# Down-projection weights loaded with two neighbouring rows per partition, and the transposes of the hidden rows read every second column

## The reference

```python
xe = jax.vmap(lambda hb, ib: hb[ib])(h, idx)              # the rows that the expert chose
a = jnp.einsum('becd,edf->becf', xe, w_gate)              # w_gate (16, 1024, 1024)
u = jnp.einsum('becd,edf->becf', xe, w_up)                # w_up   (16, 1024, 1024)
ye = jnp.einsum('becf,efd->becd', jax.nn.silu(a) * u, w_down) * gate[..., None]
```

## Time and profile before

| | before |
|---|---|
| median of three executions | 2377.05 us |
| profiled execution, first to last instruction | 2376.4 us |
| TensorE busy | 2258.4 us (95%) |
| VectorE busy | 1758.0 us (74%) |
| ScalarE busy | 1272.3 us (54%) |
| DMA, whole kernel | 529.15 MB in 167652 packets |
| mixtures (without their edges) | about 745 to 1350 us and 1755 to 2350 us |

### The profile page before, as it was taken

One profiled execution on the slowest core, in us unless ns is written; L12 is line 12 of the kernel. 1 busy time (PEld: TensorE's weight loads), 2 busy tenths in 40 slices (PEclk: granted clock), 3 DMA queues, 4 the chain that ended last, 5 costly groups with the idle time before them and its releaser, 6 DMA issues.

```text
span 2376.4 us, 27238 instructions
## 1 busy us (share of the span) xinstructions
PE 2258.4 (95%) x10012; PEld 1547.3 (65%) x10012; DVE 1758.0 (74%) x1949; ACT 1272.3 (54%) x1348; POOL 194.6 (8%) x226
## 2 busy tenths in 40 slices
PE   7999999999988999999999798999979999999995
PEld 2867868768654666666666455777646666666663
DVE  4684765757767898999999534545378989999996
ACT  4212212213135777787777434444457778877773
POOL 1000000000022010111000110000120101110001
PEclk9999999999998999999999899999999999999997
DMA  7533434525345999999999310001269999999991
GB/s 271 159 117 115 142 107 158 159 92 166 107 177 205 341 354 348 364 360 342 350 339 360 117 39 1 36 1 37 98 235 346 352 345 359 362 354 343 338 353 59
DMA packets 167652, 529.15 MB, mean 223 GB/s; under 512 B 13525, under 2 KB 22282, under 8 KB 167306
## 3 DMA queue, kind: packets, MB, share of 16 engines
q1 hardware_dynamic: 162954, 515.35, 60.4%
q0 software_dynamic: 2304, 8.39, 1.0%
q10 hardware_dynamic: 2304, 4.20, 0.5%
HBM read 516.72 MB, written 11.17 MB: 222 GB/s over the span
## 4 chain that ended last, share of the span: by engine, by line
PE 90%; DVE 4%; ACT 3%; issue 1%; POOL 1%; DMA 0%; SPq 0%; POOLq 0%; ACTq 0%; DVEq 0%
PE ps L1751 86%; PE ps L1754 4%; ACT W_HI L338 0%; DVE IDX L1446 0%; DVE B L1273 0%; DVE X L1274 0%; ACT W L338 0%; DMA REGION<-in_ada_b_dram 0%; DVE MIXREG L1445 0%; ACT B L766 0%; POOL SMALL L608 0%; DVE ROUTE L1448 0%; ACT QN_HI L338 0%; POOL SMALL L607 0%; ACT GATE L940 0%
## 5 line engine op out<-in xcount | busy, mean ns | idle before, releaser
L1483 DVE TENSOR_TENSOR W_LO<-RAW_W,W_HI 128x2048 fp32r<-128x2048 f32 x384 | 867.4, 2287 | 76.3 <-ACT W_HI L338 72.5
L338 ACT ACTIVATE W_HI<-RAW_W 128x2048 fp32r<-128x2048 f32 x384 | 726.4, 1916 | 193.2 <-PE ps L1751 192.2
L1751 PE MATMUL ps<-W_HI,XET_HI 128*80 128x512 f32 x1024 | 322.3, 396 | 7.4 <-DVE B L1517 5.8
L1751 PE MATMUL ps<-W_HI,XET_LO 128*80 128x512 f32 x1024 | 319.7, 394 | 0.0
L1751 PE MATMUL ps<-W_LO,XET_HI 128*80 128x512 f32 x1024 | 319.5, 393 | 0.0
L1751 PEld LDWEIGHTS ps<-W_HI,XET_HI 128*80 128x80 f32 x1024 | 150.9, 148 | 89.1 <-DVE B L1517 6.7
L1751 PEld LDWEIGHTS ps<-W_LO,XET_HI 128*80 128x80 f32 x1024 | 152.0, 148 | 85.8 <-issue 1.0
L1751 PEld LDWEIGHTS ps<-W_HI,XET_LO 128*80 128x80 f32 x1024 | 151.9, 148 | 84.6 <-issue 0.9
L1230 DVE SCALAR_TENSOR_TENSOR ADA_SUM<-ADA_RAW,NCOL,ADA_SUM 128x512 f32<-128x512 f32 x280 | 191.2, 745 | 0.2 <-DMA ADA_RAW<-in_ada_w_dram 0.2
L1751 PE MATMUL ps<-W_HI,HTE_HI 128*80 128x512 f32 x512 | 167.0, 407 | 8.6 <-issue 8.6
L1751 PE MATMUL ps<-W_LO,HTE_HI 128*80 128x512 f32 x512 | 161.2, 396 | 0.0
(11 more groups left out here) (270 smaller groups left out, 3480.7 us busy)
## 6 DMA issues: line engine op xcount, KB each, us to landing
RAW_W<-in_moe_w_gate_dram SPq DMA_DIRECT2D x128, 1024.0 KB, 5.6
RAW_W<-in_moe_w_up_dram SPq DMA_DIRECT2D x128, 1024.0 KB, 6.0
RAW_W<-in_moe_w_down_dram SPq DMA_DIRECT2D x128, 1024.0 KB, 5.2
ADA_RAW<-in_ada_w_dram SPq DMA_DIRECT2D x80, 512.0 KB, 3.6
RING_RAW<-in_ret_w_in_dram SPq DMA_DIRECT2D x48, 512.0 KB, 4.7
W<-in_ada_w_dram SPq DMA_DIRECT2D x4, 2048.0 KB, 14.2
RING_RAW<-in_ret_w_out_dram SPq DMA_DIRECT2D x16, 512.0 KB, 4.7
xn_rows<-B SPq DMA_DIRECT2D x8, 512.0 KB, 12.7
```

The lines of the kernel that those rows point to most:

```text
L338: return nc.scalar.activation(out, in_, ACT.Copy, scale=scale)
L1483: V_.tensor_tensor(W_LO[:, slot], RAW_W[:, slot], W_HI[:, (place + i) % HSLOTS].bitcast(F32), ALU.subtract).then_inc(MS_["lo"], 1)
L1751: return T.matmul(out, lhsT, rhs, start=first, stop=last)
```

## The change

The load of a down unit takes its rows in another order: row 256q + 2p + k goes to partition p, block k. Two neighbouring rows of the matrix, 8192 bytes in a row in HBM, now go to one partition. Gate and up units are loaded as before. To match it, transpose c of `hidden_tr` reads the columns of `HID` that belong to the rows of its half unit: 256(c // 2) + 2p + c % 2 for p from 0 to 127, every second column of a block of 256. What is summed is the same, in another order.

```diff
@@ mix_load
-                src = a[("moe_w_gate", "moe_w_up", "moe_w_down")[w]][layer].rearrange("e (q k p) n -> e q p k n", p=P, k=2)
+                rows = "e (q p k) n -> e q p k n" if w == 2 else "e (q k p) n -> e q p k n"
+                src = a[("moe_w_gate", "moe_w_up", "moe_w_down")[w]][layer].rearrange(rows, p=P, k=2)
@@ hidden_tr
                     pe.wait_ge(MS_["h"], b["h"] + e + 1)
+                    pairs = HID[0:ROWS, :].rearrange("r (q p k) -> r q k p", p=P, k=2)
                     for c in range(KD):
-                        last = tr(ps[:, 6 + c // 4, (c % 4) * ROWS:(c % 4 + 1) * ROWS], HID[0:ROWS, c * P:(c + 1) * P], ROWS)
+                        last = tr(ps[:, 6 + c // 4, (c % 4) * ROWS:(c % 4 + 1) * ROWS], pairs[:, c // 2, c % 2, :], ROWS)
```

## The result

| | before | changed |
|---|---|---|
| median of the executions | 2377.78 us (4) | 2389.19 us (4) |
| lowest to highest | 2372.39 to 2378.69 us | 2388.51 to 2390.41 us |
| profiled execution, span | 2376.4 us | 2388.6 us |

A forecast was written before the change was run, and what follows sets the result against it. TensorE was taken to bound the kernel: 2376.4 us profiled, + 0 for transposes, - 0 to 1 for loads, gives 2376, and with 0.65 us from span to median 2377 us. The range was 2369 to 2389 us.

The forecast's parts named there:

- What bounds the kernel: Mixture windows: TensorE, busy all 400 us, sets the pace; SP's load queue waited 320.7 us for it, nothing on transfers.
- The loads: 128 down loads in 8192-byte pieces: 16384 packets fewer, landing hidden with 4.6 us spare, 0 to 1 us gained.
- the 6.2 forecast: Sign in the changed profile: down loads landing after 6.2 us or less, beside other loads at 6.0.
- the 0.2 us less for each down load: Landing of each 1024 KB down load in 8192-byte pieces: 0.2 us sooner, worth nothing on the path.
- the 0.4 us: Two 2048 KB loads outside the mixtures: 7.5 us in 8192-byte pieces against 7.9 in 4096, basis for the down loads.
- The transposes: Eight per `hidden_tr`, 32 groups: strided weight load taken as zero cost under the 0.070 us pass, 0.009 us spare.
- The upper end: Stride of two halves the weight load's rate: 0.122 us, 0.052 us more for seven transposes per group, 11.6 us.
- The first rival: Strided weight load in `hidden_tr` outlasts the pass covering it; at half rate 2389 us; chance 0.13.
- The other rivals: Products relieved of load writes, 2354 or 2369 us, faster side 0.05; slower load stream becoming the bound, 2396 us, 0.02.

The follow-up runs named there:

- e4_split_on_act_and_dve: Changed kernel's paired loads, but ACT and DVE read PSUM at every second column so transposes read neighbours; 2376.39 us, ratio 0.9993 against the kernel before.

## Why the prediction was wrong

**What bounds the kernel.** Right. TensorE was busy for 400 of 400 us and SP waited for it, before and after the earlier trace rows, which is why 0.35 us added to a group of transposes came through as 0.35 us of time.

**The loads.** Right on the path: packets as forecast, no wait for them, and alone 1.0007 with an interval that holds 1. That a down load landed after 5.5 us, within the 6.2 forecast, was luck: all loads landed sooner in that window, and the forecast had the others at 6.0. No run shows the 0.2 us less for each down load, and the row behind it was weaker than I took it for. In the changed kernel the same load of 2048 KB in pieces of 8192 bytes, which the change does not touch, took as long as the one in pieces of 4096 did:

```profile
W<-in_mla_w_kv_b_dram SPq DMA_DIRECT2D x1, 2048.0 KB, 7.9
```

Over the 14 profiles of this case this load landed after 7.3 to 7.9 us and the one in pieces of 4096 bytes after 7.8 to 8.0, so the 0.4 us are partly scatter, and what is left cannot be told from the place of the two loads in the kernel. The error cost nothing, since I had given the loads no gain on the path.

**The transposes.** Here is the step that failed: "Between these ends I take zero: the nearest row is the same instruction with the same 128 columns". This put the term of the strided weight load at nothing without a row for such a read. The upper end was the truth. Its working holds term by term: a strided weight load of 0.122 us was priced and 0.120 us measured; 0.052 us more for each of seven transposes, 0.051 measured; the first one of a group hidden by a product, and hidden; 11.6 us in the sum, 11.3 in the row of the group, 11.4 in the medians. The first rival was this case at 2389 us with a chance of 0.13, and the measured 2389.19 us lie just past the range, which ended at that rival's own figure and left it no scatter.

**Why I chose the wrong end.** The 0.061 us of the earlier trace rows are the price of 128 neighbours. They say how much is spare, 0.009 us, and nothing about a spacing. I read them as the nearest row for a strided load, when no row stood nearer to one end than to the other, and "no row points to a cost" was taken for a row that shows none. The Trainium skill, "SBUF — State Buffer", the note on cachelines, pointed the same way: by it reads keep their full rate as long as each 16-byte line serves two of them. For TensorE's reads the runs disagree: numbers of 4 bytes that lie 8 bytes apart are two to a line, and the rate was about halved for a weight load (0.120 us against 0.061 us in the earlier trace rows) and for a moving operand (0.45 against 0.231 us). With 9 ns spare and no row for the operation, the two cases should have had like chances, and the text's own price of 11.6 us would have stood for one of them.

**The other rivals.** Both are out. Products in the changed kernel keep their time (394 ns in the mean of the group shown, 393 before; gate and up products start 0.230 us apart in the median in both kernels), so there was nothing to relieve; and from 850 to 1250 us no engine waited for a transfer, so the stream did not become the bound.

## What to carry to other kernels

Give TensorE neighbouring columns of float32, as weights and still more as the moving operand; where an order has to be made, make it in an ACT or DVE instruction that is there anyway (`e4_split_on_act_and_dve` did it for nothing). Before changing the shape of a weight load, compare it with the pass ahead: behind a product of 512 columns even a load at half the rate is free, behind a short transpose each ns over the pass is paid. And an operation without a row in the trace gets no price of zero when what covers it has a few ns to spare.

## What was not expected of the hardware

- Spacing in TensorE's weight loads of float32 has nearly one price: with spacings of 2, 3, 4 and 8 columns a weight load of 128 columns behind a short pass takes 0.104 to 0.120 us instead of at most 0.069 us, and with a spacing of zero it stays within that 0.069 us.
- The same spacing of two on reads of PSUM by ACT and DVE costs nothing (1026 against 1025 ns, 1210 against 1210 ns for 80x1024).
- A plain float32 product with 128 columns as weights and 128 moving columns ran as two instructions, 112 ns each, where a transpose of the same weights with 80 moving columns is one of 69 ns, and the kernel's transposes with 128 moving columns are one of 109 ns (median distance between starts).
